# Convolutions and heads of an encoder layer: from one merged order to a planned order for each engine

## The reference

```
y = h @ w_in, depthwise convolution of width 3 over q, k and the three Hyena parts
Hyena (512 channels):  z = x1 * (long_conv(v, k0) + d0 * v);  out = x2 * (long_conv(z, k1) + d1 * z)
   long_conv = irfft(rfft(z, 2L) * k, 2L)[:L]
mLSTM (4 heads x 128), forwards and backwards:
   within a chunk:  Sm = (q k^T) * exp(D - m);   across chunks: a decayed state C = sum k v^T, n = sum k
   h = (inter * q C + Sm v) / max(|den|, exp(-m));  heads are RMS-normed, scaled by a gain and sigmoid(o)
x = x + concat(Hyena, mLSTM) @ w_out;   then a gated MLP and a final norm
```

## Time and profile before

| | |
|---|---|
| median of three runs | 2577.33 us (2574.67 to 2578.0) |
| profiled execution | 2579.32 us, its span 2577.7 us, mean granted clock of TensorE 0.958 |
| the stage of the change | 772.3 us (first instruction) to 1203.6 us (first DMA of the next stage) |
| TensorE, VectorE, ScalarE, GpSimd busy in the span | 2315.3, 1181.1, 772.1, 148.0 us |

### The profile page before, as it was taken

One profiled execution on the slowest core, in us unless ns is written; L12 is line 12 of the kernel. 1 busy time (PEld: TensorE's weight loads), 2 busy tenths in 40 slices (PEclk: granted clock), 3 DMA queues, 4 the chain that ended last, 5 costly groups with the idle time before them and its releaser, 6 DMA issues. The chain is left out here.

```text
span 2577.7 us, 26949 instructions
## 1 busy us (share of the span) xinstructions
PE 2315.3 (90%) x10340; PEld 1878.6 (73%) x10340; DVE 1181.1 (46%) x1584; ACT 772.1 (30%) x1117; POOL 148.0 (6%) x164
## 2 busy tenths in 40 slices
PE   5999999998986898885886999999999993998997
PEld 3778788886864676664665788888888882787786
DVE  5675775446532776654235333333333333323332
ACT  4423322244433335433124222222221112212321
POOL 0211211000101100000000000000000000000000
PEclk9999999999998999997997999999999996999999
DMA  4344444434438667545241111111111113434442
GB/s 124 102 143 128 138 129 149 147 106 123 136 102 286 185 205 207 159 109 159 87 156 49 50 53 56 57 57 57 57 57 57 57 41 110 135 101 136 145 134 76
DMA packets 207474, 294.14 MB, mean 114 GB/s; under 512 B 13816, under 2 KB 142200, under 8 KB 207130
## 3 DMA queue, kind: packets, MB, share of 16 engines
q1 hardware_dynamic: 194842, 243.41, 32.2%
q0 software_dynamic: 11392, 46.41, 4.9%
q10 hardware_dynamic: 1152, 3.15, 0.3%
HBM read 201.09 MB, written 65.87 MB: 104 GB/s over the span
## 5 line engine op out<-in xcount | busy, mean ns | idle before, releaser
L128 PE MATMUL up_acc<-up_h_hi,up_w_hi 128*128 128x512 f32 x1056 | 412.1, 390 | 3.1 <-DVE up_w_lo L323 3.1
L129 PE MATMUL up_acc<-up_h_lo,up_w_hi 128*128 128x512 f32 x1056 | 411.8, 390 | 0.0
L130 PE MATMUL up_acc<-up_h_hi,up_w_lo 128*128 128x512 f32 x1056 | 411.7, 390 | 0.0
L245 DVE SCALAR_TENSOR_TENSOR up_u<-up_acc,up_conv_par,up_u 128x1023 f32<-128x1023 f32 x88 | 85.4, 1012 | 463.4 <-ACT up_u L311 463.4
L128 PE MATMUL down_acc<-down_w_hi,down_s_hi 128*128 128x512 f32 x528 | 209.3, 396 | 54.1 <-DVE down_w_lo L489 41.2
L128 PEld LDWEIGHTS up_acc<-up_h_hi,up_w_hi 128*128 128x128 f32 x1056 | 198.9, 188 | 44.7 <-issue 3.4
L130 PEld LDWEIGHTS up_acc<-up_h_hi,up_w_lo 128*128 128x128 f32 x1056 | 198.8, 188 | 41.4
L129 PEld LDWEIGHTS up_acc<-up_h_lo,up_w_hi 128*128 128x128 f32 x1056 | 199.0, 188 | 41.2
L311 ACT ACTIVATE up_u<-up_acc,up_conv_par 128x1536 f32<-128x1536 f32 x44 | 72.0, 1635 | 516.6 <-PE up_acc L130 516.6
L129 PE MATMUL down_acc<-down_w_lo,down_s_hi 128*128 128x512 f32 x528 | 208.0, 394 | 0.0
L130 PE MATMUL down_acc<-down_w_hi,down_s_lo 128*128 128x512 f32 x528 | 207.6, 393 | 0.0
(11 more groups left out here) (236 smaller groups left out, 3865.8 us busy)
## 6 DMA issues: line engine op xcount, KB each, us to landing
down_s_raw<-g_scratch SPq DMA_DIRECT2D x24, 1408.0 KB, 6.8
in_w_raw<-arg_w_in_t SPq DMA_DIRECT2D x58, 512.0 KB, 3.7
up_w_raw<-arg_w_up_t SPq DMA_DIRECT2D x44, 512.0 KB, 3.5
g_scratch<-up_prod POOLq DMA_DIRECT2D x22, 768.0 KB, 3.5
filt_tab<-arg_fwd SPq DMA_DIRECT2D x32, 512.0 KB, 3.8
mix_classes<-mix_split SPq DMA_DIRECT2D x48, 256.0 KB, 5.2
mix_kf<-k_scratch SPq DMA_DIRECT2D x48, 256.0 KB, 2.9
mix_split<-mix_classes SPq DMA_DIRECT2D x48, 256.0 KB, 4.8
```

Of the source, the lines that this page charges most:

```text
L128: pe.matmul(out, w_hi, x_hi, start=first, stop=False)
L129: pe.matmul(out, w_hi, x_lo, start=False, stop=False)
L130: return pe.matmul(out, w_lo, x_hi, start=False, stop=last)
L245: dve.scalar_tensor_tensor(u[:, t0 + 1:t0 + n], acc[:, t0:t0 + n - 1], w_prev, u[:, t0 + 1:t0 + n], ALU.mult, ALU.add).then_inc(half_step, 1)
```

## The change

`plan` gets an argument `even`. Where it is set, of the open steps that could start at the same time it takes the one whose stream has the smallest share done, and between steps of one kind the smaller one. Without it the order is as it was.

`long_convolutions_and_heads` no longer builds `conv`, `heads` and `schedule`. It describes its steps to the planner: `outer` is the order of splits, joins and turns, `inner` that of the heads' TensorE steps, both in the order in which they stood, and further streams hold the loads, shuffles, copies, products, norms and masks. `work` gives each step its engine, its duration, the delay until its result is there (DMAs: 4.0 to 6.0 us) and the steps it needs, buffers to come free among them. All engines now walk `order`. Some steps become finer: an attend is one step per direction, scaling keys is one per tile, turning keys and scores are two steps, and the gather of classes back into split tiles is one step per block. `load_k`, `load_gate`, `load_tab` and `load_head` are steps of their own, where before they hung on a forward, a join or a split. SP first issues z of streams 0, 2 and 3 by hand, with the outer tables behind z of stream 0, then the constants; the first `load_head` is no longer issued by hand but in the planned order. Instructions, tiles and buffers are otherwise the same.

```diff
               [N_KINDS - 1] + MIX_V_O + list(range(N_QK))]
 
 
-def plan(streams, work):
+def plan(streams, work, even=False):
 
 
 
@@ -677,15 +677,16 @@
...
         for n, stream in enumerate(streams):
             if at[n] == len(stream):
                 continue
-            engine, time, delay, needs = work(stream[at[n]])
+            step = stream[at[n]]
+            engine, time, delay, needs = work(step)
             if all(x in done for x in needs):
                 start = max([clock.get(engine, 0.0)] + [done[x] for x in needs])
-                if best is None or start < best[0]:
-                    best = start, n, engine, time, delay
+                rank = at[n] / len(stream) if even else 0
+                if best is None or (start, rank) < best[:2] or (start, rank) == best[:2] and step[0] == best[3][0] and step < best[3]:
+                    best = start, rank, n, step, engine, time, delay
         if best is None:
             break
-        start, n, engine, time, delay = best
-        step = streams[n][at[n]]
+        start, rank, n, step, engine, time, delay = best
         at[n] += 1
         clock[engine] = start + time
         done[step] = start + time + delay
@@ -1627,8 +1628,7 @@
...
     pairs = [(o, st, t) for o, st in turns for t in range(n_tiles[streams[st][0]])]
     last_pair = {(o, st): max(g for g, pair in enumerate(pairs) if pair[:2] == (o, st)) for o, st in turns}
     first_pair = {(o, st): min(g for g, pair in enumerate(pairs) if pair[:2] == (o, st)) for o, st in turns}
-    lag, ring = 2, 3
-    turn_at = {(0, 0): 12, (0, 2): 16, (0, 3): 20, (1, 0): 28, (1, 2): 32, (1, 3): 36}
+    ring = 3
...
-    conv = []
...
-    share = (sum(x[1] for x in heads) - gaps) / sum(x[1] for x in conv if x[0] != "gap")
...
 
     jobs = [(h, s) for h in range(HEADS) for s in range(len(SEQS))]
     quad, W = 4, HD + 1
@@ -1648,141 +1648,169 @@
         nt = nts[s]
         return [x for i in range(nt // 2) for x in (nt // 2 - 1 - i, nt // 2 + i)]
 
+    def joined(o, st):
+
         nb = len(blocks(st))
+        out = []
         for b in range(nb + 2):
             if b < nb:
+                out.append(("join", o, st, b))
             if b >= 2:
+                out.append(("split", 1, st, b - 2) if o == 0 else ("turn", st, b - 2))
+        return out
+
+    def splits(st):
+        return [("split", 0, st, b) for b in blocks(st)]
+
+    outer = [x for st in (0, 2, 3) for x in splits(st)]
+    for turn in ((0, 0), (0, 2), (0, 3), (1, 0)):
+        outer += joined(*turn)
+    outer += splits(1)
+    for turn in ((1, 2), (1, 3), (0, 1), (1, 1)):
+        outer += joined(*turn)
 
     def keys_of(j):
+        return [x for i in range(nts[jobs[j][1]] // quad) for x in (("turn_k", j, i), ("score", j, i))]
+
+    inner = keys_of(0)
     for j in range(len(jobs)):
         nt = nts[jobs[j][1]]
+        inner += [("link", j, i) for i in range(nt - 1)] + [("attend", j, i, d) for i in range(nt) for d in range(DIRS)]
+        inner += (keys_of(j + 1) if j + 1 < len(jobs) else []) + [("turn_head", j, i) for i in range(nt // quad)]
+
+    def bank_of(step):
+        return {"turn_k": "a", "score": "b", "turn_head": "b"}.get(step[0]) or ("bc"[step[2] % 2] if step[0] == "link" else "ac"[step[3]])
+
+    def freed(step):
+
+        kind, a = step[0], step[1:]
+        return {"turn_k": ("scale_keys",) + a + (quad - 1,), "score": ("weigh",) + a, "link": ("add_state",) + a, "attend": ("combine",) + a,
+                "turn_head": ("scale",) + a, "split": ("copy_split",) + a, "join": ("finish",) + a, "turn": ("copy_turned",) + a}[kind]
+
+    older = {step: outer[n - 2] for n, step in enumerate(outer) if n >= 2}
+    for name in "abc":
+        uses = [x for x in inner if bank_of(x) == name]
+        older.update({x: y for x, y in zip(uses[1:], uses)})
+    same_slot = {(o, st): [x for x in turns if (x[1] < 2) == (st < 2)] for o, st in turns}
+
+    def gate_before(o, st):
+        n = same_slot[o, st].index((o, st))
+        return same_slot[o, st][n - 1] if n else None
+
+    def last_block(turn):
+        return turn + (len(blocks(turn[1])) - 1,)
+
+    def work(step):
+
+        kind, a = step[0], step[1:]
+        free = [freed(older[step])] if step in older else []
+        if kind == "load_z":
+            return "SP", 0.6, 5.0, [("turn", 0, len(blocks(0)) - 1)] if a[0] == 1 else []
         if kind == "split":
+            return "PE", 0.9, 0, [("finish", 0) + a[1:] if a[0] else ("load_z", a[1])] + free
+        if kind == "copy_split":
+            return "ACT", 0.65, 0, [("split",) + a]
+        if kind == "to_classes":
+            return "SP", 0.7, 5.5, [("copy_split",) + a] + ([("store_turned", 0)] if a == (0, 1, 0) else [])
+        if kind == "load_tab":
+            return "SP", 0.6, 6.0, []
+        if kind == "load_k":
+            return "SP", 0.6, 4.0, [("multiply", a[0] - ring)] if a[0] >= ring else []
+        if kind == "forward":
+            o, st, t = pairs[a[0]]
+            return "PE", 0.9, 0, [("to_classes", o, st, b) for b in blocks(st)] + [("load_tab", streams[st][0])] + (
+                [("multiply", a[0] - 2)] if a[0] >= 2 else [])
+        if kind == "multiply":
+            return "DVE", 2.1, 0, [("forward", a[0]), ("load_k", a[0])] + ([("inverse", a[0] - 2)] if a[0] >= 2 else [])
+        if kind == "inverse":
+            return "PE", 1.8, 0, [("multiply", a[0])] + ([("copy_classes", a[0] - 1)] if a[0] else [])
+        if kind == "copy_classes":
+            return "ACT", 0.65, 0, [("inverse", a[0])]
+        if kind == "to_split":
+            return "SP", 0.7, 5.5, [("copy_classes", last_pair[a[:2]])]
+        if kind == "join":
+            return "PE", 0.9, 0, [("to_split",) + a[:2] + (b,) for b in blocks(a[1])] + free
+        if kind == "load_gate":
+            before = gate_before(*a)
+            return "SP", 0.6, 5.0, [("finish",) + last_block(before)] if before else []
+        if kind == "finish":
+            return "DVE", 0.5, 0, [("join",) + a, ("load_gate",) + a[:2]]
+        if kind == "turn":
+            return "PE", 0.25, 0, [("finish", 1) + a] + free
+        if kind == "copy_turned":
+            return "ACT", 0.85, 0, [("turn",) + a]
+        if kind == "store_turned":
+            return "ACT", 0.3, 4.0, [("copy_turned", a[0], len(blocks(a[0])) - 1)]
+
+        j = a[0]
+        nt = nts[jobs[j][1]]
+        if kind == "load_head":
+            return "SP", 3.0, 4.5, [("attend", j - 2, nt - 1, 1)] if j >= 2 else []
+        if kind == "mask":
+            return "POOL", nt / 2, 0, [("load_head", j)]
+        if kind == "weigh_tile":
+            return "ACT", 0.8, 0, [("mask", j)]
+        if kind == "turn_k":
+            return "PE", 0.5, 0, [("load_head", j)] + free
+        if kind == "score":
+            return "PE", 1.0, 0, [("load_head", j)] + free
+        if kind == "scale_keys":
+            return "ACT", 0.8, 0, [("turn_k",) + a[:2]] + ([("link", j - 1, nts[jobs[j - 1][1]] - 2)] if j else [])
+        if kind == "weigh":
+            return "DVE", 1.5, 0, [("score",) + a] + [("weigh_tile", j, quad * a[1] + x) for x in range(quad)]
+        if kind == "link":
+            return "PE", 0.6, 0, [("scale_keys", j, nt // quad - 1, quad - 1)] + free
+        if kind == "add_state":
+            before = nts[jobs[j - 1][1]] // quad - 1 if j else None
+            return "DVE", 0.75, 0, [("link",) + a] + ([("turn_head", j - 1, before)] if j and a[1] == 0 else [])
+        if kind == "attend":
+            return "PE", 0.6, 0, [("weigh", j, nt // quad - 1), ("add_state", j, nt - 2)] + free
+        if kind == "age":
+            return "ACT", 0.4, 0, [("attend",) + a]
+        if kind == "combine":
+            return "DVE", 0.4, 0, [("attend",) + a] + ([("age",) + a] if carried(a[2], jobs[j][1], outwards(jobs[j][1])[a[1]]) else [])
+        if kind == "magnitude":
+            return "ACT", 0.35, 0, [("combine", j, nt - 1, DIRS - 1)]
+        if kind == "shares":
+            return "DVE", 0.6, 0, [("magnitude", j)]
+        if kind in ("weight", "add", "square", "reduce"):
+            return "DVE", 0.2 + 0.14 * nt, 0, []
+        if kind == "root":
+            return "ACT", 1.6, 0, [("reduce", j)]
+        if kind == "unit":
+            return "DVE", 0.4 + 0.14 * nt, 0, [("root", j)]
+        if kind == "turn_head":
+            return "PE", 0.5, 0, [("unit", j)] + free
+        if kind == "load_o":
+            return "SP", 0.6, 4.0, [("store_head", j - 2)] if j >= 2 else []
+        if kind == "scale":
+            return "DVE", 0.8, 0, [("turn_head",) + a, ("load_o", j)]
+        return "SP", 0.6, 4.0, [("scale", j, nt // quad - 1)]
+
+    of_jobs = range(len(jobs))
+    by_tile = [(j, i) for j in of_jobs for i in range(nts[jobs[j][1]])]
+    by_quad = [(j, i) for j in of_jobs for i in range(nts[jobs[j][1]] // quad)]
+    aged = [(j, i, d) for j, i in by_tile for d in range(DIRS) if carried(d, jobs[j][1], outwards(jobs[j][1])[i])]
```

(45 more changed lines are left out.)

283 lines of the change are left out of this document (70 added, 213 removed).

## The result

The changed kernel takes 2594.94 us in the median of four runs (2590.42 to 2596.68), the one before 2577.66 beside it (2574.67 to 2579.25): 1.0066 times as long, interval 1.0048 to 1.0083. It is slower by 17 us, where 23 less were forecast; that is less than 1%, but clear of the scatter between runs. The profiled execution took 2593.6 us.

A forecast was written before the change was run, and what follows sets the result against it. No engine is full in the convolution and head stage; TensorE idles 91.2 of 431.3 us in waits. Terms 0 - 10 - 9 - 7 + 3 = -23 us gave 2556.3, by the median 2554.3 us; range 2518 to 2588.

The forecast's parts named there:

- Start: 772 to 861 us: longer wait for the first head and earlier first forward cancel; 0, bounds -12 and +25.
- the offset set against the wait: Start: first forward at 815 to 828, leftover work fills the second stretch, whose idle and half clock vanish; -12 us.
- Middle: 861 to 1068.7 us: step-by-step order places ready head steps in PE's waits; -10 us, bounds 0 and -22.
- pairs further apart than 3.4 us: Sign that the forecast is wrong: convolution pairs in the middle spaced more than 3.4 us.
- Last stream: 1068.7 to 1164.6 us: last turn's forward no longer waits behind a head's links and attends; -9 us, bounds 0 and -19.
- tail: 1164.6 to 1203.6 us: joins no longer wait behind the last head's attends; -7 us, bounds 0 and -16.
- The two waits that were named: Stage's end: last turn's forward 9 us late, its joins 6 us late, both behind head work.
- Given back: Head work moved out of the end must lie elsewhere, and real durations differ from the plan's; +3 us, bounds 0 and +14.
- VectorE beside GpSimd's mask: Wide squares meeting a mask on the shared port cost about 2 us each; up to 8 us worse, left at 0.
- The first head comes late: Rival: table and gates pass ahead of the first head, PE waits, the chain shifts; +25 at start, 2592 us, chance 0.20.
- Only the place changes: Rival: head work taken from the end returns as waits in the middle; 2575 to 2579 us, chance 0.10.
- The denser stage: Rival: PE reaches 91% busy from the first forward on; -51 us, 2526 us, chance 0.20.

The follow-up runs named there:

- e9: The kernel before, engine order unchanged, with SP's first loads in the changed kernel's order: 2589.5 us, 1.0037 of the kernel before.
- e7: The changed kernel with the planner's durations and DMA delays both set nearer the trace, nothing else: 2578.2 us, 0.9999 of the kernel before.
- e12: e8 with norm steps 0.5 us apart in the plan and heads counted 0.05 less far along in ties: 2564.06 us, 0.9946 of the kernel before.
- e8: e7 with the load order of e2, second table and head after stream 0's last gather, output gates after forwards: 2567.16 us, 0.9953 of the kernel before.
- e2: The changed kernel with the first head loaded right after the constants, z2 and z3 behind it, gates after the first forward: 2596.38 us, 1.0070.

## Why the prediction was wrong, step by step

*Start, taken as 0.* This is the first step that failed. The landing was priced right: 803 to 825 predicted, 804.25 measured, the wait 17.02 in 15 to 37. The Trainium skill ("DMA: Bandwidth & Descriptors", section on queues, rings and completion order) says that each DMA engine takes the descriptors of one ring in order, and the trace agrees roughly: the head, issued behind table and gates, landed 34.55 us after the stage's start. In this stretch 337 GB/s moved, 11.6 MB where the prediction had counted 10.6, so about 1 MB of what was issued behind the head went with it. What failed is the offset set against the wait. The first forward was put at 815 to 828 and came at 830.67. Its last gather went out at 815.75 only, since the split copy in front of it stood behind the first head's work in ScalarE's list, and it took 14.8 us to land behind the second head and the second table. I followed PE's and SP's lists, but neither ScalarE's nor what SP issues behind the first head. The term is +13.7 us of idle time; e9 shows 10.7 for the loads alone, in the old order.

*Middle, taken as -10.* From the first forward to the split of stream 1 PE idles 10.3 us more, so this step failed in sign. I took the greedy order as good because it places a ready step, and the window 600 to 700 as its proof. But "ready" is by the plan's clock, which has the first forward 31 us after the start where it comes after 61, and from there on all engines walk in an order made for other times. e7 shows that the plan's numbers are the cause of most of the loss: with durations and delays nearer the trace the same planner idles 12.6 us less behind the start. By which waits the wrong numbers cost the time stays open, since in e7 too the first forward comes 31 us later than planned. The pairs further apart than 3.4 us that were named as a sign are there, beside the norm in one piece (inverse transforms at 868.77 and 878.91). What I did not see is that steps without needs are taken in a block.

*Last stream, taken as -9, and tail, taken as -7.* The two waits that were named went. The joins start 0.1 us after the last shuffle landed (1199.4) instead of 7 us after, and the tail is 32.5 us instead of 39.0: -6.5, as forecast. The stream's term was mis-sized. From the last gather's issue to the forward 8.8 us pass instead of 15.3, and the forward starts when that gather has landed. But it took 8.7 us to land, and 7.1 in the kernel before, not the 5.2 of the median that I used; and 1.9 us came back between that forward and the tail (29.1 us before, 30.9 after). So from the last gather to the tail it is -4.6. Against -16 forecast for both, -11 came.

*Given back, +3.* About 6 us of work moved out of the end into the second line of the table: above the +3, within the bound of +14. The rest of the +29.5 us there is 13.2 of the first head's work, left over from the start, and 10.3 idle time. By these terms the stage's 19 us are 13.7 (start) + 10.3 (middle) - 11 (end) + 6 (moved work).

*VectorE beside GpSimd's mask, left at 0.* The slow squares did not become more: the four wide squares took 2.59 us each in the mean before and 1.22 in the changed kernel, and VectorE was busy 243.9 us instead of 247.9. That VectorE was quicker there bought no time in the stage.

*The rivals.* "The first head comes late" gave 2592, and 2595 was measured. Its mechanism is in the trace: PE stands at the head's keys with two split blocks behind it, and these hold the last two gathers. Its prices are not. It had a wait of 37 us where 17 was measured, and a loss of 25 at the start where 13.7 came; it did not have the second half of the loss, the plan's own numbers, and its decision point, a landing of 815, was wrong, since with 804 the loss was there already. That its sum is within 3 us of the measured time is luck. "Only the place changes" holds for the work of the end alone. The denser stage did not come in any form: from the first forward on, PE was to be 91% busy, and it is 82% in the kernel before (304.5 of 371.0), 81% in the changed one (317.3 of 389.5) and 84% in e12 (307.0 of 365.8).

*Open.* How the 17 us that e7 wins divide between durations and delays, and at which steps they are won: each alone moves 1 to 5 us. And why blocks of norm steps cost 25 us in the old order, while e7, with seven of eight norms still in a block, loses nothing.

## What to carry to other kernels

A planned order is only as good as the durations and arrival times it is planned with: compare the plan's own time of a few milestones with the trace before believing it, and try corrected durations and delays together, since each alone moved almost nothing here. At this stage's start loads landed by the bytes in front of them in the queue, not after a fixed delay, so put on the queue first what the first chain needs, and keep everything else behind it (e8; in e2, with the plan's old numbers, this alone won nothing). When two orders are compared, compare the work done by a milestone and not only its time.

## What was not expected of the hardware

At the start of the stage the DMA engines are full: share 0.99 at 294 GB/s over 60.9 us in the changed kernel, 1.00 at 279 over 46.2 in e8. Before, 40 us at a share of 0.98 moved 358 GB/s, so a full share is no fixed rate. A v of 512 KB takes 12.5 us to land there and 8.9 in the median of the three later ones; a gather of 256 KB took up to 14.8 us there, and 3.2 in the median once the start was over. The granted clock of the first stretch fell from 0.78 to 0.70 with its emptier PE, and the stage's from 0.92 to 0.89.
